# adaLN gates in a two-layer trunk on one core: chunk sums by 32x32 folds on VectorE, gates spread to all partitions by DMA

## What is computed

```python
def reference(x, c, ada_w, ada_b, ...):          # x (1, 256, 2048), c (1, 2048), fp32
    c_act = silu(c)
    for i in range(2):
        mod = c_act @ ada_w[i] + ada_b[i]        # ada_w[i] (2048, 12288)
        sh_mix, sc_mix, g_mix, sh_mlp, sc_mlp, g_mlp = split(mod, 6)
        h = modulate(rmsnorm(x, norm_mix[i]), sh_mix, sc_mix)
        mix = fox_mixer(h, ...) if i == 0 else short_conv_mixer(h, ...)
        x = x + g_mix * mix
        h = modulate(rmsnorm(x, norm_mlp[i]), sh_mlp, sc_mlp)
        x = x + g_mlp * (square(relu(h @ w_up[i])) @ w_down[i])
    return rmsnorm(x, final_norm)
```

## Time and profile before

| | |
|---|---|
| three runs | 2309.1, 2310.5 (median), 2312.11 us |
| the profiled execution, from its first to its last instruction | 2308.7 us |
| mean granted TensorE clock | 0.998 |
| busy: PE, PEld, DVE, ACT, POOL | 2261.7, 1923.2, 1694.9, 1085.0, 173.0 us |
| share of the span | 98%, 83%, 73%, 47%, 7% |
| chain that ended last, by engine | PE 89%, DVE 5%, DMA 2%, issue 2% |
| moved | 615.65 MB, mean 267 GB/s |

### The profile page before, as it was taken

One profiled execution on the slowest core, in us unless ns is written; L12 is line 12 of the kernel. 1 busy time (PEld: TensorE's weight loads), 2 busy tenths in 40 slices (PEclk: granted clock), 3 DMA queues, 4 the chain that ended last, 5 costly groups with the idle time before them and its releaser, 6 DMA issues.

```text
span 2308.7 us, 29983 instructions
## 1 busy us (share of the span) xinstructions
PE 2261.7 (98%) x11704; PEld 1923.2 (83%) x11704; DVE 1694.9 (73%) x1634; ACT 1085.0 (47%) x1232; POOL 173.0 (7%) x339
## 2 busy tenths in 40 slices
PE   6999999999999999999999999999999999999998
PEld 5999998778888888888887888887888888888886
DVE  6888999968857967967977888866885555555555
ACT  4444444464435435435545444446443543543553
POOL 0001111101101101101100111100110000000000
PEclk9999999999999999999999999999999999999999
DMA  9987999959958968968977888855985566556563
GB/s 364 386 314 256 334 350 338 392 183 319 330 192 293 346 219 289 334 235 273 330 249 244 315 311 317 322 186 182 318 297 188 186 197 188 189 190 199 183 209 120
DMA packets 270534, 615.65 MB, mean 267 GB/s; under 512 B 14705, under 2 KB 15041, under 8 KB 269505
## 3 DMA queue, kind: packets, MB, share of 16 engines
q1 hardware_dynamic: 220480, 437.56, 55.3%
q0 software_dynamic: 46080, 167.79, 20.2%
q10 hardware_dynamic: 3840, 8.42, 1.1%
HBM read 611.62 MB, written 2.10 MB: 266 GB/s over the span
## 4 chain that ended last, share of the span: by engine, by line
PE 89%; DVE 5%; DMA 2%; issue 2%; ACT 1%; SPq 0%; DVEq 0%; ACTq 0%
PE ps L511 19%; PE ps L513 18%; PE ps L512 18%; PE ps L499 16%; PE ps L500 8%; PE ps L486 2%; PE ps L487 2%; PE ps L488 2%; DMA start_ring<-in_ada_w_dram 2%; DVE acc L1431 1%; DMA ada_raw<-in_ada_w_dram 1%; DVE hb L1431 1%; DVE w_lo L1411 1%; PE ps L555 0%; DVE square_out L1431 0%
## 5 line engine op out<-in xcount | busy, mean ns | idle before, releaser
L912 ACT ACTIVATE w_hi<-raw 128x1024 fp32r<-128x1024 f32 x721 | 762.8, 1060 | 986.7 <-PE ps L513 710.9
L1411 DVE TENSOR_TENSOR w_lo<-raw,w_hi 128x1024 fp32r<-128x1024 f32 x721 | 878.1, 1222 | 467.0 <-ACT w_hi L912 465.5
L499 PE MATMUL ps<-h,w_hi 128*128 128x512 f32 x1536 | 541.4, 398 | 0.0
L511 PE MATMUL ps<-w_hi,mid 128*128 128x512 f32 x1280 | 501.4, 392 | 0.8 <-DVE mid L1754 0.8
L513 PE MATMUL ps<-w_lo,mid 128*128 128x512 f32 x1280 | 498.3, 389 | 0.0
L512 PE MATMUL ps<-w_hi,mid 128*128 128x512 f32 x1280 | 498.0, 389 | 0.0
L500 PE MATMUL ps<-h,w_lo 128*128 128x256 f32 x1536 | 430.4, 280 | 0.0
L499 PEld LDWEIGHTS ps<-h,w_hi 128*128 128x128 f32 x1536 | 288.5, 188 | 71.6 <-DVE w_lo L1411 0.6
L511 PE MATMUL ps<-w_hi,h 128*128 128x512 f32 x756 | 299.0, 396 | 9.2 <-DVE h L1567 8.8
L513 PE MATMUL ps<-w_lo,h 128*128 128x512 f32 x756 | 294.7, 390 | 0.0
L512 PE MATMUL ps<-w_hi,h 128*128 128x512 f32 x756 | 294.3, 389 | 0.0
(11 more groups left out here) (248 smaller groups left out, 1800.4 us busy)
## 6 DMA issues: line engine op xcount, KB each, us to landing
ada_raw<-in_ada_w_dram POOLq DMA_DIRECT2D x320, 512.0 KB, 6.4
raw<-in_mlp_w_up_dram SPq DMA_DIRECT2D x128, 1024.0 KB, 5.3
raw<-in_mlp_w_down_dram SPq DMA_DIRECT2D x128, 1024.0 KB, 5.8
raw<-in_fox_w_in_dram SPq DMA_DIRECT2D x48, 1024.0 KB, 10.2
raw<-in_conv_w_in_dram SPq DMA_DIRECT2D x48, 1024.0 KB, 7.5
start_ring<-in_ada_w_dram SPq DMA_DIRECT2D x64, 512.0 KB, 12.2
raw<-in_fox_w_out_dram SPq DMA_DIRECT2D x16, 1024.0 KB, 10.8
raw<-in_conv_w_out_dram SPq DMA_DIRECT2D x16, 1024.0 KB, 5.1
```

What stands on the lines that cost most here:

```text
L499: mm(o, hi[:, jc], both, start=(k == 0), stop=False, skip_group_check=True)
L511: mm(o, xh, hi, start=(k == first), stop=False)
L912: op(w_hi[:, e % WR], raw[:, e // 2, EK * (e % 2):EK * (e % 2 + 1)], ACT.Copy).then_inc(hi_ready, 1)
L1411: v.tensor_tensor(w_lo[:, e % WR], raw[:, e // 2, EK * (e % 2):EK * (e % 2 + 1)], w_hi[:, e % WR].bitcast(F32), ALU.subtract).then_inc(spl ...
```

## The change

All 20 chunks are folded on VectorE. For the chunks 0, 1, 2 and 5 that is the path the other shift and scale chunks had. For a gate half, TensorE's matmul has `acc_part` as weights and 32 columns of `fold`, which gives a 32x32 block with the 1024 sums in row order (L555 of the changed kernel). VectorE adds the bias to it in `gate_parts` (L1494). ScalarE's queue writes the block, 4 KB, to a row in DRAM, `gate_rows` (`gate_write`, L972, in 32 runs of 128 B; it waits for `mod_ready`), and loads that row broadcast to 128 partitions into its half of `gate`, 512 KB (`gate_load`, L978; it waits for the write and for the residual adds that still use the old gate). Eight writes and eight loads take the place of four loads of 1 MB. The biases come in at the start by four loads into `gate_parts`, ahead of ScalarE's first activation. `add_gated` now waits for the load's `gate_arrived` of that half. `ones` shrinks to one column. The sums and stores of chunks 3 and 4 stand at the usual places, and chunk 1 of a slice one pair earlier than before.

```diff
-FOLDED = [i for i, (b, _) in enumerate(ADA) if PARTS[b] not in GATE and i >= A_MLP0]
+FOLDED = list(range(len(ADA)))
...
-        ones = sb("ones", [P, P])
+        ones = sb("ones", [P, 1])
...
+        gate_parts = sb("gate_parts", [BLK, len(GATE) * NH, NA // BLK])
+        gate_rows = nc.dram_tensor("gate_rows", [len(GATE) * NH, NA], F32).ap()
...
-        QKV_SUM, QKV_STORE = sums_of(PLAN_QKV, {3: (8 * U_OUT0 + 5, 8 * U_OUT0 + 6), 4: (8 * U_OUT0 + 15, 8 * U_OUT0 + 16),
-                                                 5: (8 * U_OUT0 + 22, 8 * U_OUT0 + 23)})
-        SLICE_SUM, SLICE_STORE = sums_of(PLAN_SLICE)
+        QKV_SUM, QKV_STORE = sums_of(PLAN_QKV, {5: (8 * U_OUT0 + 22, 8 * U_OUT0 + 23)})
+        SLICE_SUM, SLICE_STORE = sums_of(PLAN_SLICE, {1: (PLAN_SLICE[1][1] + 3, PLAN_SLICE[1][1] + 4)})
...
                     pe.wait_ge(acc_folded, folded_before(i) + 1)
+                    if is_gate:
+                        mm(ps[0:NA // BLK, SUM, 0:BLK], acc_part[:, :], fold[:, 0:BLK], start=True, stop=True).then_inc(ada_summed, 1)
+                        return
                     mm(ps[:, SUM, 0:NA // BLK], fold[:, :], acc_part[:, :], start=True, stop=True).then_inc(ada_summed, 1)
...
-                if is_gate:
-                    for b in range(2):
-                        last = mm(ps[:, SUM - 1 + b, :], ones[:, :], accs[slot][:, NU * b:NU * (b + 1)], start=True, stop=True)
...
+            for (layer, part), g in GATE.items():
+                act.dma_start(gate_parts[:, NH * g:NH * (g + 1), :],
+                              ada_b[layer, D * part:D * (part + 1)].rearrange("(n j r) -> j n r", j=NA // BLK, r=BLK)
+                              ).then_inc(gate_bias_arrived, 16)
+
             act.wait_ge(c_step, 1)
             op(ce[:, 0, :], c_col[:, :], ACT.Exp, scale=-1.0).then_inc(c_exp, 1)
+
+            def gate_write(i, g, n):
+
+                act.wait_ge(mod_ready, i + 1)
+                act.dma_start(gate_rows[NH * g + n].rearrange("(j r) -> j r", r=BLK), gate_parts[:, NH * g + n, :]).then_inc(gate_written, 16)
+
+            def gate_load(g, n, n_added):
+
+                act.wait_ge(gate_written, 16 * (NH * g + n + 1))
+                act.wait_ge(added, n_added)
+                act.dma_start(gate[:, NA * n:NA * (n + 1)], gate_rows[NH * g + n:NH * g + n + 1, :].broadcast_to([P, NA])
+                              ).then_inc(gate_arrived[n], 16)
...
+                if u == 3 * NG - 1:
+                    after[6] = lambda: gate_write(A_GATE0, 0, 0)
...
                 residual(at(U_OUT0 + n), n, R_OUT0, 1,
-                         (None, {3: load_root}, None, None)[n],
-                         first=None if n else {0: lambda: round_probs(NG - 1), 4: first_gate})
+                         ({4: lambda: gate_load(0, 0, 0)},
+                          {3: lambda: [load_root(), gate_write(A_GATE0 + 1, 0, 1)], 5: lambda: gate_load(0, 1, 0)}, None, None)[n],
...
-                        hooks[5] = lambda: load_gate(l, gate_part, r0)
...
+                        also(final, {3: lambda: gate_write(first_ada + half, g, half), 5: lambda: gate_load(g, half, r0)} if half else
+                             {2: lambda: gate_write(first_ada, g, 0), 4: lambda: gate_load(g, 0, r0)})
...
-            def gate_store(i, n, n_gate):
+            def gate_store(i, n, g):
                 dve.wait_ge(ada_summed, i + 1)
-                dve.wait_ge(gate_arrived, 16 * n_gate)
-                half = gate[:, NA * n:NA * (n + 1)].rearrange("p (b n) -> p b n", b=2)
-                v.tensor_tensor(half, ps[:, SUM - 1:SUM + 1, :], half, ALU.add).then_inc(mod_ready, 1)
+                dve.wait_ge(gate_bias_arrived, 16 * len(GATE))
+                rows = gate_parts[:, NH * g + n, :]
+                v.tensor_tensor(rows, ps[0:NA // BLK, SUM, 0:BLK], rows, ALU.add).then_inc(mod_ready, 1)
...
-                first = {R_OUT0: A_GATE0, R_MLP0: A_MLP0, R_OUT1: A_CONV, R_MLP1: A_MLP1}.get(r)
-                if first is not None:
-                    dve.wait_ge(mod_ready, first + n // 2 + 1)
+                g = {R_OUT0: 0, R_MLP0: 1, R_OUT1: 2, R_MLP1: 3}.get(r)
+                if g is not None:
+                    dve.wait_ge(gate_arrived[n // 2], 16 * (g + 1))
```

More of the change, by code:

```diff
@@ L372, in folded_before @@
                 return sum(c < i for c in FOLDED)
-            return i - (A_MLP0 + NH)
+            return i - (A_MLP0 + NH - sum(c < A_MLP0 + NH for c in FOLDED))
         def sums_of(plan_, overrides={}):
@@ L552, in ada_sum @@
                 pe.wait_ge(ada_steps, KC * (i + 1))
[L553 to L559 removed]
+                for j in range(2 * NB):
+                    last = mm(ps[:, SUM, j:j + 1], accs[slot][:, P * j:P * (j + 1)], ones[:, 0:1],
+                              start=True, stop=True)
                 last.then_inc(ada_summed, 1)
```

38 lines of the change are left out of this document (19 added, 19 removed).

## The result

The changed kernel takes 2318.6 us (median of 5 runs, 2313.43 to 2321.07) against 2310.5 before (5 runs, 2309.02 to 2312.11): ratio 1.0029, interval 1.0018 to 1.0040. It is slower by 0.2 to 0.4%, not faster by 0.18%. The profiled execution has a span of 2316.8 us, 8.1 over that of before, which is also the distance of the two medians. Three executions, one of the kernel before (2510.65 us), one of the run mods_only (8349.27) and one of the run before_wait (2822.98), were far slower (mean clock 0.415 and 0.751 in the last two), and no ratio, mean or interval here has them.

The account below looks back on a forecast made before the run. TensorE was taken as the bound after 510 us, both TensorE and VectorE as full from 200 to 456 us. Terms +4.5 + 0.3 - 9.0 = -4.2 us gave 2306.3 us (-0.18%), range 2302.5 to 2315.0.

Parts of the forecast that it names:

- TensorE's saving per sum: TensorE's sums: folding saves 1.50 us per gate half and 1.55 us per shift or scale chunk.
- After 510 us: -9.0: Late stages, six gate halves: VectorE's lead hides the folds, TensorE keeps 6 x 1.50 = 9.0 us.
- I cost it at nothing: After 510 us: VectorE's extra 1.5 us per gate half hides in 162 us of its idle time.
- 200 to 456 us: +4.5: Early stage, chunks 0 to 5: VectorE gets 14.6 us more, waits absorb 8.6, chunk 5's sum is 1.55 cheaper.
- all 6.0 pass on to it: End of chunk 5's fold: VectorE's 6.0 us of lateness reaches TensorE in full, as it already waited there.
- rival 2: Near 456 us: a TensorE wait of 4 to 5 us lowers its clock, costing 3.4 us, 2309.7 in all; chance 0.11.
- Start: +0.3: Kernel start: four added bias loads cost 0 to 1.9 us, taken as +0.3.
- 4 x 0.47: Start, ScalarE's queue: issuing the four bias loads takes 1.9 us ahead of its table load.
- the cover of 2.49 us: Start: VectorE's 2.49 us wait for the first adaLN tile was to hide the bias loads' issue time.
- rival 4: Gate loads landing in 12.2 us come late for residual adds, costing 8.2 us, 2314.5 in all; chance 0.09.
- Rival 1: Early stage: folds hidden throughout, all twelve sums' savings stay, 2292.6 us; chance 0.05.
- Rival 3: Early stage: VectorE's waits absorb nothing, stage costs +13.1, 2314.9 us, or 2316.5 with the start's upper bound; chance 0.15.

Follow-up runs that it names:

- mods_only: Changed kernel with chunks 3 and 4 (gate 0) summed and loaded as before, chunks 0, 1, 2 and 5 still folded: ratio 1.0034, 2318.81 us.
- before_wait: Kernel before, with two unused reductions of 1.2 us each added on VectorE ahead of `mid` in unit 6: ratio 1.0023, 2317.48 us.
- best: Changed kernel with chunks 0 to 5 as before, the three bias loads in unit 9, chunk 14's fold one slot later: ratio 0.9968, 2304.5 us.
- spin_all: Changed kernel with idle matmuls ahead of all five long TensorE waits of the early stage: ratio 1.0008, 2313.61 us.
- bias_late: Changed kernel with the four bias loads issued in unit 9 instead of at the start: ratio 1.0018, 2315.94 us.
- fold0_later: Changed kernel with chunk 0's fold on VectorE moved behind the next w_lo and the two subtractions that write mid and vs: ratio 1.0013, 2314.44 us.
- late_only: Changed kernel with chunks 0 to 5 summed and stored as before, only the six later gate halves folded and spread by DMA: ratio 0.9986, 2308.9 us.
- best2: As best, but gate 0 (chunks 3 and 4) folded and spread by DMA too: ratio 0.9972, 2305.36 us.

## Why the prediction was wrong, step by step

Measured is 12.3 us above the forecast. By stage of the two profiles: +5.3 in the early stage (7.0 of clock that the sum did not have; without it the stage costs 2.8, not the 4.5 of the forecast), +2.6 in the late savings, +2.0 at the start, and +2.4 at two places that do not follow the change.

- **TensorE's saving per sum.** Right in kind, 10% too large: a late gate half gives 1.36 us, not 1.50. The new sum was priced by a folded sum's 0.22 and costs 0.38.
- **After 510 us: -9.0.** The mechanism was right, and in full for four of the six halves. The profile has -2.72 - 1.0 - 2.72 = -6.4: four halves at 1.36, the convolution's second at 1.36 less a new 0.5, its first at 0.15. "I cost it at nothing" failed there. For the first, best shows that the place, not the length of the fold, was the reason (1.30 with the fold one slot later); the 0.5 of the second stays in best, and its cause is open. 0.92 us more stand mostly in unit 46, where VectorE waited 1.8 us for an adaLN tile (1.0 before), ahead of a fold that both kernels have; 1.46 us stand in a loop turn, where the profile of before was faster than in its other turns (last section).
- **200 to 456 us: +4.5.** The part on VectorE was sized well. 4.4 + 1.2 + 0.8 = 6.4 us of the waits on `w_hi` were forecast to stay. In spin_all, where the clock stays up to 465 us, VectorE's waits on `w_hi` from 202 to 468 us are 6.3 us. In the changed kernel they are 9.5, since TensorE at the lower clock frees the slots late: one wait of 4.3 at 253 us, which is 1.2 in mods_only, where the clock did not fall there, and 5.9 in before_wait and bias_late, where it lost 5.1. The failed words are "all 6.0 pass on to it" at chunk 5. The lateness reached TensorE at five places, in waits of 1.8 to 3.4 us, of which the first comes from the two instructions of chunk 0's fold ahead of `mid` (fold0_later). The savings of TensorE between them only made the waits longer, as the text said.
- **The clock, rival 2 (0.11).** This is the step that decided: the sum has no term for it. It was put at one wait near 456 us, at 3.4 us, and held unlikely because the clock of the stretch from 456 to 510 stood at 1.00 with 3.6 us of idle time. That 1.00 was one execution's: late_only and best have a fall in that stretch with waits as short. In the runs the clock's part is 4.9 to 5.8 us in the mean (spin_all; the clock of the runs), spread over several waits, and before_wait shows the cause alone: 2.2 us more of one wait, 3.5 us of clock in the mean of the runs, 5.2 in its profile. Without those 5.8 us the changed kernel would stand at 2312.8, inside the stated range, and still slower than before. The Trainium skill's page "TensorE: Matmul & The Clock Gate" (Part 1, the HAM clock gate) says that an idle TensorE falls to 1.2 GHz. By that rule the rival held, and the trace agrees in part: 0.50, the lower level, in a window behind before_wait's 2.7 us, and 0.83 and 0.91 in windows behind waits of 2.2 to 3.4 us of the changed kernel. But its waits of 2.4 and 1.8 us had no fall behind them, nor had the 3.0 of mods_only.
- **Start: +0.3.** Wrong, +2.34 in the profile; the profiles with a bias load behind `wf` have +2.2 to +3.3, those without it +0.2 to +0.5 (bias_late, best, best2). "4 x 0.47" took the issue price of a queue with room. The first issue behind `wf` took 7.26 us, and the cover of 2.49 us was gone.
- **The gate's trip, rival 4.** Did not happen: no wait for `gate`; the landings of up to 9.0 us reach the bound of 9 for an odd half, but not over it. The median of 7.5 is above the 5.0 that was taken for twice the bytes, which is itself a median (one of those four loads took 9.5). The writes, which had 5.4, took 5.3 at most.
- **Rivals 1 and 3.** Rival 1 fell: TensorE waits 13.8 us from 205 to 480 us, where it waited 2.1. Rival 3 came nearest, 2314.9 and up to 2316.5, for a wrong reason: the waits did absorb. That it is near is luck.

The sum without the clock is +2.3 + 2.8 - 6.4 = -1.3 us (2.8 is 9.84 less the 7.0 of the clock); the +8.1 of the profile is that, plus 7.0 for the clock, plus 0.92 and 1.46 at the two places named above.

## What to carry to other kernels

Where TensorE is nearly always busy, cost a new wait of it at its own length and at what the clock takes behind it: here 2.2 us more of waiting went with 3.5 us of lower clock in the mean of eight executions. Extra work on a helper engine belongs behind the operand that TensorE asks for next, and only in stages where the helper has time; a fold was worth -1.36 us late, and chunk 0's had cost 4.1 us by unit 7 in the changed kernel's profile, 3.4 of them clock. A DMA issue is cheap only on a queue with room: look at what the load ahead of it has in runs, and keep such issues away from the first instruction that the start waits for.
